# Input projection's head: one small load on ACT, the first norm's gains turned alone, the first weight tile split in halves, addresses moved by 128 bytes

## The chip, the cores and the metric

The kernel runs on one core of one Trainium2 chip. The metric is device time in microseconds of one execution of the whole program; the time before is the median of three runs, 1946.9 us (1945.45 to 1949.15).

## The reference, cut to what matters

One layer of a streaming encoder: a prompt of 1024 tokens and 8 samples of 16 tokens, width 1024, all in float32. The change touches only the first step, the norm and the projection into 3336 columns:

```python
def rmsnorm(x, g):
    xf = x.astype(jnp.float32)
    y = xf * lax.rsqrt(jnp.mean(xf * xf, axis=-1, keepdims=True) + EPS)
    return (y * g.astype(jnp.float32)).astype(x.dtype)

xn = rmsnorm(x, lw['norm_mix_g'])
(qkv_raw, z, a, b, sq, sk, sv, sc_b, sc_c, sc_h) = split_cols(xn @ lw['w_in'], IN_SIZES)
```

After it come the gated delta rule, a window attention, a short convolution, the output projection, an attention into 256 memory tokens and the feed-forward part; none of their code changes.

## The kernel before, in words

Tokens: 1152 rows (1024 of the prompt, 128 of the samples) lie as 9 row tiles of 128 rows (x0 to x8 below), in three groups of three. Each product is computed as three float32r matmuls, from a high and a low part of either factor (`w_hi`·`hi`, `w_hi`·`lo`, `w_lo`·`hi`, lines 920 to 923).

`in_projection` (line 646) walks over 25 column tiles of the weights; the first five are sc_c, sc_h, sc_b, sc_c, sc_h. A column tile has three pieces (one for each group of 384 tokens), a piece has 8 inner blocks k, and a block three matmuls, "a product" below. Tile 0 does the norm at the same time. The steps of this head, by engine:

- SP (lines 728 to 738) issues the loads in one fixed order: x0, x1, x2, weights 0, x3, x4, x5, weights 1, x6, x7, x8, the two halves of the feed-forward convolution's old rows (16 rows of 2816 floats each, at partitions 0 to 15 and 32 to 47), the old rows of the two other convolutions, and then, each after a split of weights, weights 2 and on.
- ACT (lines 1013 to 1016) first issues 18 small loads, all vectors of the layer (14 in `table`, 4 in `vectors`), then loads its table, and runs `InputNorm.on_scalar` (line 310): the sums of squares of x0, x1, x2 (`square`), one square root for the three (`lengths`), and then, for each of 24 blocks i = 8·group + k, `high_part(i)`. After blocks 0, 1, 2 come the squares of x3, x4, x5, and after 8, 9, 10 those of x6, x7, x8 (`SPREAD`).
- PE (line 906) first waits for all 18 small loads and turns them into columns (`turn_vectors`, line 788), then turns the 8 blocks of the first group (`first_third`), each of three transposes into one of four PSUM banks: block i waits until block i−4 is through `low_part`. Then tile 0's products begin; before product k of piece p, PE turns block 8p + k + 4 (`before_product`, line 272) and waits for the low part of its own block. After piece 0 and 1 it turns the old feed-forward rows, after piece 2 the other old rows (`beside`, line 880).
- DVE (line 1287) copies the turned vectors into `C.vec`, then runs `on_vector` (line 324): the reciprocal and three scalings of group 0 (`scale`), then 24 times `low_part`; before blocks 4 and 12 it scales groups 1 and 2, before blocks 12 and 20 it copies old feed-forward rows out. Only then it splits weights 2 (`weights_low`).
- POOL (line 1087) makes the identity, splits weights 0 (a copy and a subtraction over the whole tile), makes the masks and splits weights 1.

Every engine runs its instructions in this order; semaphores alone join them. SBUF tiles on the left side lie one behind the other in the order in which `program` (line 4322) makes them; weights of this projection lie on the right side.

Of the kernel before, what the change touches and what calls it, by code (L numbers as in the profile page):

```python
# [11 lines left out]
F32 = mybir.dt.float32  # L12
F32R = mybir.dt.float32r
ALU = mybir.AluOpType
# [3 lines left out]
P = 128  # L18
# [70 lines left out]
class Ctx:  # L89


    def __init__(self, nc, stack):
        self.nc, self.stack = nc, stack
# [105 lines left out]
class NormParts:  # L199
# [4 lines left out]
    def __init__(self, nc, C, ph, tag, src, sums, gain_col, hi, lo, xn, banks):  # L204
        self.nc, self.C, self.src, self.sums, self.gain_col = nc, C, src, sums, gain_col
        self.hi, self.lo, self.banks = hi, lo, banks
        self.xn = xn.rearrange("p (i t d) -> p i t d", i=2, t=self.GROUP)
        self.root, self.inv = (ph.sb(f"{tag}_{n}", [P, NT]) for n in ("root", "inv"))
# [71 lines left out]
class InputNorm(NormParts):  # L280


    SPREAD = {0: 3, 1: 4, 2: 5, 8: 6, 9: 7, 10: 8}

    def __init__(self, nc, C, ph, src, hi, lo, xn, banks, squares, landed, ready):
        super().__init__(nc, C, ph, "nx", src, C.h_sums, V_MIX, hi, lo, xn, banks)
        self.squares, self.landed, self.ready = squares, landed, ready
        self.summed, self.vec_copied = ph.sem("nx_summed"), ph.sem("nx_vec_copied")

    def square(self, act, t):  # L290
        act.wait_ge(self.landed[t], 16)
        if t:
            act.wait_ge(self.summed, t)
        self.nc.scalar.activation(self.squares, self.src[:, t, :], ACT.Square, accum_out=self.sums[:, t:t + 1]
                                  ).then_inc(self.summed, 1)

    def lengths(self, act, g):
        ts = slice(g * self.GROUP, (g + 1) * self.GROUP)
        act.wait_ge(self.summed, (g + 1) * self.GROUP)
# [10 lines left out]
    def on_scalar(self, act):  # L310
        act.wait_ge(self.ready, 1)
        for t in range(self.GROUP):
            self.square(act, t)
        self.lengths(act, 0)
        act.wait_ge(self.vec_copied, 1)
        for i in range(NP * KD):
            self.high_part(act, i)
            t = self.SPREAD.get(i)
            if t is not None:
                self.square(act, t)  # L320
                if t % self.GROUP == self.GROUP - 1:
                    self.lengths(act, t // self.GROUP)

    def on_vector(self, dve, copy_old):
        self.scale(dve, 0)
        dve.wait_ge(self.vec_copied, 1)
        for i in range(NP * KD):
            if i % KD == KD // 2:
                if i // KD:
                    copy_old(i // KD - 1)  # L330
                if i // KD + 1 < NP:
                    self.scale(dve, i // KD + 1)
            self.low_part(dve, i)


class Ahead:
# [153 lines left out]
class FeatureWeights:  # L490
# [155 lines left out]
def in_projection(nc, C, A, O, M, hi, lo, weights, spill, scratch, x_tiles):  # L646
# [20 lines left out]
    with C.phase() as ph:  # L667
# [28 lines left out]
        x_landed = [ph.sem(f"x_landed{t}") for t in range(NT)]  # L696
        x_rows = kv.rearrange("p a b -> p (a b)").rearrange("p (t d) -> p t d", d=D)
        norm = InputNorm(nc, C, ph, x_rows, hi, lo, mix_flat[:, 0:6 * D],
                         [sums[:, i, :] for i in range(NP)] + [state_out[:]], R.x_squares, x_landed, ready)
        table, vectors = vector_table(C, A, *R.vec_rows)  # L700
        staged = ph.sem("c_staged")
        stored = C.conv_stored
        (rows_landed, projected, act_freed, dve_freed, old_turned, old_copied, padded, conv_step, conv_done,
# [20 lines left out]
        def _(sp):  # L724
# [60 lines left out]

        @block.tensor
        def _(pe):
            def turn_vectors():
                pe.wait_ge(ready, 1)
                pe.wait_ge(loaded, 16 * (len(table) + len(vectors)))  # L790
                at = 0
                for rows in R.vec_rows:
                    n = rows.shape[0]
                    ins = nc.tensor.transpose(misc[:, at:at + n], rows, C.ident[0:n, 0:n])
                    at += n
                ins.then_inc(vec_turned, 1)

# [22 lines left out]
            def turn_state(m):  # L820

                W = 3 if m < 2 else 4
                pe.wait_ge(gathered, m + 1)
                if m:
                    pe.wait_ge(state_saved, m)
                nc.tensor.transpose(state_out[0:W - 1, 0:P], tail[:, m % 2, 24:24 + W - 1], C.ident[:])
                nc.tensor.transpose(state_out[0:NB * (W - 1), P:2 * P], tail[:, m % 2, 0:NB * (W - 1)],
                                    C.ident[:]).then_inc(state_turned, 1)
# [51 lines left out]
            def beside(n, piece):  # L880

                if n == 0:
                    if piece < 2:
                        turn_ffn_rows(piece)
                    else:
                        turn_old_rows()
                if piece == 0:
                    if n >= 1 and tiles[n - 1][0] == "sc_h":
                        turn_state(tiles[n - 1][1])
                if piece == 1:  # L890
                    if n >= 1 and tiles[n - 1][0] == "conv":
                        turn_state(padded_of["conv", tiles[n - 1][1]])
                    if n == FIRST:
                        turn_gates()
                    if n == FIRST + 1:
                        sum_gates()
                    if n == FIRST + 2:
                        turn_gc()
                    if 0 <= n - FIRST - 2 < 2 * HEADS:
                        sum_squares(n - FIRST - 2)  # L900
                for e in KK_AT.get((n - COVER, piece), ()):
                    kk(e)
                if 0 <= NP * (n - COVER) + piece - 4 < E_ALL:
                    turn_v(NP * (n - COVER) + piece - 4)

            turn_vectors()
            norm.first_third(pe)
            for n, (kind, i, cols) in enumerate(tiles):
                rows = sum(c for _, c in cols)
                pe.wait_ge(split, n + 1)  # L910
                for piece in range(NP):
                    if n:
                        if by_act[n - 1]:
# [3 lines left out]
                    for k in range(KD):  # L917
                        if n == 0:
                            norm.before_product(pe, piece, k)
                        for m, (w, x) in enumerate(((w_hi, hi), (w_hi, lo), (w_lo, hi))):  # L920
                            ins = nc.tensor.matmul(banks[0:rows, piece, 0:TC], w[:, n % 2, k, 0:rows],  # L921
                                                   x[:, k, piece * TC:piece * TC + TC], start=(k == 0 and m == 0),
# [9 lines left out]
        def _(act):  # L932
# [127 lines left out]
        def _(pool):  # L1060
# [63 lines left out]
        def _(dve):  # L1124
# [162 lines left out]
            dve.wait_ge(vec_turned, 1)  # L1287
            nc.vector.tensor_copy(C.vec[:], misc[:, 0:V_ALL]).then_inc(norm.vec_copied, 1)
# [3033 lines left out]
def program(nc, A, O):  # L4322
    with ExitStack() as stack:
# [155 lines left out]
```

## Time and profile before

| | |
|---|---|
| median of three runs | 1946.9 us |
| profiled execution | 1941.18 us |
| its span, first to last instruction | 1939.8 us |
| PE busy | 1851.0 us (95%) |
| DVE, ACT, POOL busy | 60%, 41%, 38% |
| mean granted clock of PE | 0.988 |

The span is what the trace covers; some 1.4 us of the profiled execution lie around it. Busy times of an engine are shares of that span. PE is busy nearly everywhere, so what matters is where it is not.

### The profile page before, as it was taken

The page shows a single profiled execution, that of the slowest core. Times are in us where ns is not written, and L with a number is a line of the kernel's source. Part 1 is how long each engine was busy: PE and PEld are TensorE (multiplying, and loading weights), DVE is VectorE, ACT ScalarE, POOL GpSimd, SP SyncE. Part 2 cuts the span into 40 slices and gives each one's busy share as a digit, 9 for nine tenths or more (in the row PEclk, how much of TensorE's full clock was granted, in tenths as well). Part 3 has the DMA queues.
Part 4 walks back from the last instruction along what each step waited for, and adds up shares of the span by engine and source line. Part 5 has one row for each costly group of instructions (what it writes and reads, how often), then busy time and mean ns, then how long its engine had stood idle before and what let it go on. Part 6 is the DMA issues. An engine that isn't in the chain of part 4 may idle for free. (4 is left out here: it accounts for less than half of the span.)

```text
span 1939.8 us, 27945 instructions
## 1 busy us (share of the span) xinstructions
PE 1851.0 (95%) x10427; PEld 1694.0 (87%) x10427; DVE 1162.3 (60%) x1367; ACT 788.0 (41%) x1499; POOL 737.4 (38%) x650
## 2 busy tenths in 40 slices
PE   5999999999989999999998997999999999999999
PEld 4989889998967788898887887999999999987787
DVE  4224555655656642423415148887788877699985
ACT  4104664315675442311124236444444444444432
POOL 3001212005434260121114305766666666547743
PEclk9999999999999999999999999999999999999999
DMA  6121212214133340112431122222222222496454
GB/s 165 36 57 35 59 35 56 70 59 138 55 120 120 120 176 22 44 66 92 172 117 55 55 66 77 77 68 68 78 68 77 69 68 68 156 340 205 160 172 142
DMA packets 159034, 188.07 MB, mean 97 GB/s; under 512 B 13809, under 2 KB 112730, under 8 KB 158520
## 3 DMA queue, kind: packets, MB, share of 16 engines
q1 hardware_dynamic: 157156, 186.30, 29.2%
q8 instruction: 65, 1.06, 0.2%
q10 hardware_dynamic: 884, 0.25, 0.1%
q0 software_dynamic: 896, 0.19, 0.0%
q14 instruction: 33, 0.27, 0.0%
HBM read 151.64 MB, written 35.07 MB: 96 GB/s over the span
## 5 line engine op out<-in xcount | busy, mean ns | idle before, releaser
L3573 PE MATMUL ffn_banks<-h_parts,up_hi 128*128 128x384 f32 x1920 | 496.5, 340 | 10.0 <-POOL h_parts L3977 4.3
L3573 PEld LDWEIGHTS ffn_banks<-h_parts,up_hi 128*128 128x128 f32 x1920 | 350.2, 189 | 11.4 <-issue 7.2
L3573 PE MATMUL ffn_banks<-h_parts,up_lo 128*128 128x384 f32 x960 | 325.4, 339 | 0.0
L3973 POOL TENSOR_TENSOR up_lo<-up_raw,up_hi 128x512 fp32r<-128x512 f32 x174 | 256.2, 1489 | 141.6 <-ACT up_hi L3735 141.5
L921 PE MATMUL proj_banks<-x_hi,in_w_hi 128*128 128x384 f32 (+1 forms) x648 | 225.6, 348 | 4.2 <-DVE room L1308 4.2
L921 PE MATMUL proj_banks<-x_lo,in_w_hi 128*128 128x384 f32 (+1 forms) x648 | 220.1, 340 | 0.0
L921 PE MATMUL proj_banks<-x_hi,in_w_lo 128*128 128x384 f32 (+1 forms) x648 | 219.8, 339 | 0.0
L3573 PEld LDWEIGHTS ffn_banks<-h_parts,up_lo 128*128 128x128 f32 x960 | 181.1, 189 | 0.0
L4024 POOL TENSOR_TENSOR h_parts<-down_cells,h_parts 128x512 fp32r<-128x512 f32 x69 | 111.0, 1616 | 92.7 <-ACT h_parts L3808 92.6
L3694 PE MATMUL ffn_banks<-h_parts,up_hi 128*128 128x512 f32 x352 | 140.0, 398 | 0.8 <-DVE h L4241 0.8
L3697 PE MATMUL ffn_banks<-h_parts,up_lo 128*128 128x512 f32 x352 | 138.9, 395 | 0.0
L3696 PE MATMUL ffn_banks<-h_parts,up_hi 128*128 128x512 f32 x352 | 138.8, 394 | 0.0
L921 PEld LDWEIGHTS proj_banks<-x_hi,in_w_hi 128*128 128x128 f32 (+1 forms) x648 | 120.5, 186 | 8.1 <-DVE in_w_lo L783 4.8
L3735 ACT ACTIVATE up_hi<-up_raw 128x512 fp32r<-128x512 f32 x176 | 105.3, 630 | 47.2 <-DVE up_raw L4052 37.8
L921 PEld LDWEIGHTS proj_banks<-x_lo,in_w_hi 128*128 128x128 f32 (+1 forms) x648 | 120.4, 186 | 3.1
L921 PEld LDWEIGHTS proj_banks<-x_hi,in_w_lo 128*128 128x128 f32 (+1 forms) x648 | 120.1, 185 | 2.1
L4052 DVE TENSOR_TENSOR up_raw<-up_raw 128x512 f32<-128x512 f32 x88 | 117.9, 1358 | 2.0
L1105 POOL MEMSET room<- 128x3 f32 (+1 forms) x14 | 1.4, 101 | 243.2 <-DVE room L1145 216.6
L783 DVE TENSOR_TENSOR in_w_lo<-in_w_raw,in_w_hi 128x1024 fp32r<-128x1024 f32 (+1 forms) x25 | 32.8, 1311 | 97.7 <-ACT in_w_hi L940 97.6
L4115 DVE SCALAR_TENSOR_TENSOR h<-h,vec 128x1168 f32<-128x1168 f32 x44 | 85.9, 1951 | 2.1 <-ACT h L3785 2.1
L4119 DVE SCALAR_TENSOR_TENSOR h<-h,vec 128x1168 f32<-128x1168 f32 x44 | 81.0, 1841 | 5.8 <-DVE h L4115 2.4
L3820 ACT ACTIVATE up_hi<-up_raw 128x640 fp32r<-128x640 f32 (+1 forms) x66 | 46.0, 701 | 90.1 <-DVE up_raw L4225 45.1
(515 smaller groups left out, 3918.2 us busy)
## 6 DMA issues: line engine op xcount, KB each, us to landing
up_raw<-in_w_up SPq DMA_DIRECT2D x44, 512.0 KB, 3.7
down_cells<-in_w_down SPq DMA_DIRECT2D x58, 256.0 KB, 5.7
up_raw<-ffn_gated_rows SPq DMA_DIRECT2D x44, 320.0 KB, 5.6
ffn_gated_rows<-h SPq DMA_DIRECT2D x22, 576.0 KB, 2.8
in_w_raw<-in_w_in SPq DMA_DIRECT2D x24, 512.0 KB, 3.7
up_raw<-ffn_gated_rows SPq DMA_DIRECT2D x44, 256.0 KB, 3.2
mem_k_one<-in_cache_mem_k SPq DMA_DIRECT2D x8, 1024.0 KB, 4.9
spill<-mixT SPq DMA_DIRECT2D x10, 576.0 KB, 3.8
```

What stands on the lines that cost most here:

```text
L921: ins = nc.tensor.matmul(banks[0:rows, piece, 0:TC], w[:, n % 2, k, 0:rows], x[:, k, piece * TC:piece * TC + TC], start=(k == 0 and m == 0 ...
L3573: ins = nc.tensor.matmul(banks[:, bank, 0:TC], wt[:, j, k, :], parts[:, q, x, k, :], start=(fresh and n == 1), stop=(n == last), skip_grou ...
L3694: nc.tensor.matmul(bank, a_hi[:, x_at, w_at], b_slot(n, 0), start=(i == 0 and not again), stop=False, skip_group_check=again)
L3696: nc.tensor.matmul(bank, a_hi[:, x_at, w_at], b_slot(n, 1), start=False, stop=False, skip_group_check=again)
L3697: ins = nc.tensor.matmul(bank, a_lo[:, x_at, w_at], b_slot(n, 0), start=False, stop=(i == STEPS - 1), skip_group_check=again)
L3735: nc.scalar.activation(w_hi[:, j], weights.full(j), ACT.Copy).then_inc(weights.high[j], 1)
L3820: nc.scalar.activation(a_hi[:, n % LEAD, 0:a_width(n)], a_cell(n), ACT.Copy).then_inc(a_high, 1)
L3973: nc.gpsimd.tensor_tensor(w_lo[:, j], weights.full(j), w_hi[:, j].bitcast(F32), ALU.subtract).then_inc(weights.split[j], 1)
L4024: nc.gpsimd.tensor_tensor(b_slot(n, 1), b_cell(n), b_slot(n, 0).bitcast(F32), ALU.subtract).then_inc(b_split, 1)
L4052: nc.vector.tensor_tensor(weights.full(j), x, z, op).then_inc(weights.formed[j], 1)
L4115: nc.vector.scalar_tensor_tensor(y[:, s, 0:LY], xp[:, s, 1:1 + LY], C.vec[:, col], y[:, s, 0:LY], ALU.mult, ALU.add).then_inc(conv_step, 1)
L4119: nc.vector.scalar_tensor_tensor(y[:, s, 0:LY], xp[:, s, 2:2 + LY], C.vec[:, col], y[:, s, 0:LY], ALU.mult, ALU.add).then_inc(conv[s], 1)
```

## The change

It does these things, all in the input projection's head but for the last:

1. ACT issues one load alone, the gains of this norm (`table[0]`); the other 17 small loads go to SP's queue, behind x8.
2. PE turns these gains alone (`turn_mix_gains`) before the first group; the other vectors are turned into the bank `state_out` after piece 0 of tile 1, and DVE copies them between the old rows' copy and the split of weights 2.
3. The loads of the old feed-forward rows go from behind x8 to in front of weights 1.
4. The squares are shared: ACT has x0 to x3, x5, x6, x8, DVE has x4 (after low part 1) and x7 (after low part 9).
5. DVE scales the next group before low parts 5 and 13 (was 4 and 12), and PE turns one block less ahead (k + 3 for k + 4).
6. POOL splits weights 0 in two halves of four blocks each; tile 0 starts on the first half.
7. The norm uses `C.root` and `C.inv` for its own two small tiles, and an unused tile of 128 bytes per partition, `level`, is put behind `eps`, so that the left side's later tiles lie 128 bytes higher.

```diff
+    ON_SCALAR, ON_VECTOR = {1: 3, 4: 5, 8: 6, 10: 8}, {1: 4, 9: 7}
+    SCALE_AT = KD // 2 + 1
...
+    def square_dve(self, dve, t):
+        dve.wait_ge(self.landed[t], 16)
+        if t > self.GROUP + 1:
+            dve.wait_ge(self.summed_dve, t // self.GROUP - 1)
+        self.nc.vector.scalar_tensor_tensor(self.junk, self.src[:, t, :], 1.0, self.src[:, t, :], ALU.mult, ALU.mult,
+                                            accum_out=self.sums[:, t:t + 1]).then_inc(self.summed_dve, 1)
...
         for i in range(NP * KD):
-            if i % KD == KD // 2:
-                if i // KD:
-                    copy_old(i // KD - 1)
-                if i // KD + 1 < NP:
-                    self.scale(dve, i // KD + 1)
+            if i % KD == KD // 2 and i // KD:
+                copy_old(i // KD - 1)
+            if i % KD == self.SCALE_AT and i // KD + 1 < NP:
+                self.scale(dve, i // KD + 1)
             self.low_part(dve, i)
+            t = self.ON_VECTOR.get(i)
+            if t is not None:
+                self.square_dve(dve, t)
+
+    def before_product(self, pe, p, k):
+        i = KD * p + k + KD - self.SCALE_AT
...
+    def split_halves(self, nc, pool, high, split):
+        self.wait(pool, 0)
+        for i, (to_high, to_split) in enumerate(((high, split), (self.high, self.split))):
+            ks = slice(i * KD // 2, (i + 1) * KD // 2)
+            nc.gpsimd.tensor_copy(self.hi[:, 0, ks], self.raw[:, 0, ks]).then_inc(to_high, 1)
+            pool.wait_ge(to_high, 1)
+            nc.gpsimd.tensor_tensor(self.lo[:, 0, ks], self.raw[:, 0, ks], self.hi[:, 0, ks].bitcast(F32), ALU.subtract
+                                    ).then_inc(to_split, 1)
...
-            for s in range(2):
-                sp.dma_start(ffn_rows[s], A["state_ffn_conv"][0].rearrange("b i c -> (b i) c")[:, FF * s:FF * s + FF]
-                             ).then_inc(ffn_landed, 16)
+                if n == 0:
+                    for s in range(2):
+                        sp.dma_start(ffn_rows[s], A["state_ffn_conv"][0].rearrange("b i c -> (b i) c")[:, FF * s:FF * s + FF]
+                                     ).then_inc(ffn_landed, 16)
+            for to, frm in table[1:] + vectors:
+                sp.dma_start(to, frm).then_inc(loaded, 16)
...
+            def turn_mix_gains():
+                pe.wait_ge(ready, 1)
+                pe.wait_ge(mix_landed, 16)
+                nc.tensor.transpose(misc[:, V_MIX:V_MIX + KD], table[0][0], C.ident[0:KD, 0:KD]).then_inc(mix_turned, 1)
...
                 if piece == 0:
+                    if n == 1:
+                        turn_vectors()
...
-            turn_vectors()
+            turn_mix_gains()
             norm.first_third(pe)
...
-            for to, frm in table + vectors:
-                act.dma_start(to, frm).then_inc(loaded, 16)
+            act.dma_start(*table[0]).then_inc(mix_landed, 16)
...
-            weights.split_first(nc, pool, 0)
+            weights.split_halves(nc, pool, half_high, half_split)
...
+            dve.wait_ge(vec_turned, 1)
+            nc.vector.tensor_copy(C.vec[:, mix.stop:], state_out[:, mix.stop:V_ALL]).then_inc(rest_copied, 1)
+            dve.wait_ge(rest_copied, 1)
             for n, (kind, i, cols) in enumerate(tiles):
...
+        C.sb("level", [P, 32])
```

## Rows read from the trace of the kernel before

**Rows 1.** The page's part 1: busy us (share of the span) xinstructions.
```profile
PE 1851.0 (95%) x10427; PEld 1694.0 (87%) x10427; DVE 1162.3 (60%) x1367; ACT 788.0 (41%) x1499; POOL 737.4 (38%) x650
```
**Rows 2.** PE's waits, 0 to 90 us: waited for: us, times, longest.
```profile
PE misc L794 <- DMA sinks<-in_swa_sinks: 15.9, 1, 15.9
PE proj_banks L921 <- DVE room L1308: 3.0, 1, 3.0
```
**Rows 3.** Timeline, ACT: start, us, instruction [idle before <-releaser].
```profile
8.09 0.45 ACTq L1014 DMA_DIRECT2D sinks<-in_swa_sinks  x1
8.57 1.28 ACT L1015 ACT_TABLE_LOAD   x1 [8.57 <-issue]
9.87 1.06 ACT L294 ACTIVATE room<-kv 128x1024 f32<-128x1024 f32 x1
...
13.53 0.30 ACT L300 ACTIVATE nx_root<-h_sums,eps 128x3 f32<-128x3 f32 x1
```
**Rows 4.** Timeline: the vectors' turn, then scalings, turns and high part of group 0.
```profile
15.92 0.80 PE L794 MATMUL misc<-ident,room 91*128 91x91 f32 x3 [15.92 <-DMA sinks<-in_swa_sinks]
...
17.27 2.14 DVE L226 TENSOR_SCALAR mixT<-kv,nx_inv 128x1024 f32<-128x1024 f32 x3
...
19.46 2.18 PE L239 MATMUL norm_sums<-ident,mixT 128*128 128x128 f32 x9 [2.75 <-DVE mixT L226]
...
20.46 0.58 ACT L246 ACTIVATE x_hi<-norm_sums,vec 128x384 fp32r<-128x384 f32 x1 [6.63 <-PE norm_sums L239]
```
**Rows 5.** DMA issue to landing: x0 to x2; x3 to x5; x6 to x8; weights 0; feed-forward rows.
```profile
DMA to landing us min/median/max: 3.7/4.5/6.2
...
DMA to landing us min/median/max: 9.1/9.5/10.3
...
DMA to landing us min/median/max: 11.4/12.8/12.9
...
DMA to landing us min/median/max: 8.3/8.3/8.3
...
DMA to landing us min/median/max: 11.8/13.1/14.4
```
**Rows 6.** Timeline, PE in tile 0 and at the start of tile 1.
```profile
27.07 0.67 PE L921 MATMUL proj_banks<-x_hi,in_w_hi 128*128 128x384 f32 x1
...
28.17 0.52 PE L921 MATMUL proj_banks<-x_hi,in_w_hi 128*128 128x384 f32 x1
...
34.22 1.53 PE L807 MATMUL misc<-ident,mixT 16*128 16x16 f32 x22
...
40.62 0.52 PE L239 MATMUL norm_sums<-ident,mixT 128*128 128x128 f32 x3 [1.31 <-DVE x_lo L251]
...
45.66 0.55 PE L239 MATMUL norm_sums<-ident,mixT 128*128 128x128 f32 x3
...
52.34 0.44 PE L921 MATMUL proj_banks<-x_hi,in_w_hi 128*128 128x384 f32 x1
```
**Rows 7.** Windows: stretch, PE, PEld, DVE, ACT, POOL busy, PEclk, DMA share, GB/s.
```profile
25.00:30.00 5.00, 3.68 (x15) 3.47 (x15) 4.04 (x8) 2.86 (x8) 1.35 (x1) 0.69 1.06 192
```
**Rows 8.** DMA part, 20.0 to 24.7 us, when the old rows were moved.
```profile
DMA packets 286, 0.48 MB, mean 101 GB/s; under 512 B 48, under 2 KB 238, under 8 KB 266
```
**Rows 9.** Timeline: splits of weights 0 and 2, weights 3's high part.
```profile
11.69 2.35 POOL L534 TENSOR_TENSOR in_w_lo<-in_w_raw,in_w_hi 128x1024 fp32r<-128x1024 f32 x1
...
52.94 1.23 DVE L783 TENSOR_TENSOR in_w_lo<-in_w_raw,in_w_hi 128x1024 fp32r<-128x1024 f32 x1
...
65.37 1.06 ACT L940 ACTIVATE in_w_hi<-in_w_raw 128x1024 fp32r<-128x1024 f32 x1 [12.46 <-PE proj_banks L921]
```
**Rows 10.** Groups by line: count | busy us, mean ns | idle.
```profile
L921 PE MATMUL proj_banks<-x_lo,in_w_hi 128*128 128x384 f32 (+1 forms) x648 | 220.1, 340 | 0.0
L921 PE MATMUL proj_banks<-x_hi,in_w_lo 128*128 128x384 f32 (+1 forms) x648 | 219.8, 339 | 0.0
...
L2324 DVE SCALAR_TENSOR_TENSOR swa_att<-swa_work,hide 128x1024 f32<-128x1024 f32 x9 | 11.0, 1219 | 20.4 <-PE swa_work L2224 9.1 <-PE swa_work L2229 6.0 <-PE swa_work L2226 5.3
```

More of the change, by code:

```diff
@@ L207, in __init__ @@
         self.xn = xn.rearrange("p (i t d) -> p i t d", i=2, t=self.GROUP)
-        self.root, self.inv = (ph.sb(f"{tag}_{n}", [P, NT]) for n in ("root", "inv"))
+        self.root, self.inv = C.root, C.inv
         self.rooted, self.inverted, self.scaled, self.turned, self.high, self.low = (
@@ L280, with __init__ @@
 class InputNorm(NormParts):
-    SPREAD = {0: 3, 1: 4, 2: 5, 8: 6, 9: 7, 10: 8}
-    def __init__(self, nc, C, ph, src, hi, lo, xn, banks, squares, landed, ready):
+    ON_SCALAR, ON_VECTOR = {1: 3, 4: 5, 8: 6, 10: 8}, {1: 4, 9: 7}
+    SCALE_AT = KD // 2 + 1
+    def __init__(self, nc, C, ph, src, hi, lo, xn, banks, squares, junk, landed, ready):
         super().__init__(nc, C, ph, "nx", src, C.h_sums, V_MIX, hi, lo, xn, banks)
-        self.squares, self.landed, self.ready = squares, landed, ready
-        self.summed, self.vec_copied = ph.sem("nx_summed"), ph.sem("nx_vec_copied")
+        self.squares, self.junk, self.landed, self.ready = squares, junk, landed, ready
+        self.summed, self.summed_dve, self.vec_copied = (ph.sem(f"nx_{n}") for n in ("summed", "summed_dve", "vec_copied"))
+        self.count = 0
     def square(self, act, t):
@@ L292, in square @@
         if t:
-            act.wait_ge(self.summed, t)
+            act.wait_ge(self.summed, self.count)
+        self.count += 1
         self.nc.scalar.activation(self.squares, self.src[:, t, :], ACT.Square, accum_out=self.sums[:, t:t + 1]
                                   ).then_inc(self.summed, 1)
+    def square_dve(self, dve, t):
[4 more added lines that the diff above has]
+                                            accum_out=self.sums[:, t:t + 1]).then_inc(self.summed_dve, 1)
     def lengths(self, act, g):
         ts = slice(g * self.GROUP, (g + 1) * self.GROUP)
-        act.wait_ge(self.summed, (g + 1) * self.GROUP)
+        act.wait_ge(self.summed, self.count)
+        if g:
+            act.wait_ge(self.summed_dve, g)
         self.nc.scalar.activation(self.root[:, ts], self.sums[:, ts], ACT.Sqrt, scale=1.0 / D, bias=self.C.eps[:, 0:1]
@@ L317, in on_scalar @@
             self.high_part(act, i)
-            t = self.SPREAD.get(i)
+            t = self.ON_SCALAR.get(i)
             if t is not None:
@@ L325, in on_vector @@
         self.scale(dve, 0)
-        dve.wait_ge(self.vec_copied, 1)
         for i in range(NP * KD):
-            if i % KD == KD // 2:
-                if i // KD:
-                    copy_old(i // KD - 1)
-                if i // KD + 1 < NP:
-                    self.scale(dve, i // KD + 1)
-            self.low_part(dve, i)
+            if i % KD == KD // 2 and i // KD:
+                copy_old(i // KD - 1)
+            if i % KD == self.SCALE_AT and i // KD + 1 < NP:
+                self.scale(dve, i // KD + 1)
+            self.low_part(dve, i)
+            t = self.ON_VECTOR.get(i)
[3 more added lines that the diff above has]
+        i = KD * p + k + KD - self.SCALE_AT
+        if KD <= i < NP * KD:
+            self.turn(pe, i)
+        pe.wait_ge(self.low, KD * p + k + 1)
 class Ahead:
@@ L698, in in_projection @@
         norm = InputNorm(nc, C, ph, x_rows, hi, lo, mix_flat[:, 0:6 * D],
-                         [sums[:, i, :] for i in range(NP)] + [state_out[:]], R.x_squares, x_landed, ready)
+                         [sums[:, i, :] for i in range(NP)] + [state_out[:]], R.x_squares, R.y[:, 0:D], x_landed, ready)
         table, vectors = vector_table(C, A, *R.vec_rows)
+        mix_landed, mix_turned, half_high, half_split, rest_copied = (ph.sem(f"s0_{n}") for n in (
+            "mix_landed", "mix_turned", "half_high", "half_split", "rest_copied"))
         staged = ph.sem("c_staged")
@@ L787, in _ @@
         def _(pe):
+            def turn_mix_gains():
+                pe.wait_ge(ready, 1)
+                pe.wait_ge(mix_landed, 16)
+                nc.tensor.transpose(misc[:, V_MIX:V_MIX + KD], table[0][0], C.ident[0:KD, 0:KD]).then_inc(mix_turned, 1)
             def turn_vectors():
-                pe.wait_ge(ready, 1)
-                pe.wait_ge(loaded, 16 * (len(table) + len(vectors)))
+                pe.wait_ge(loaded, 16 * (len(table) - 1 + len(vectors)))
                 at = 0
@@ L793, in turn_vectors @@
                     n = rows.shape[0]
-                    ins = nc.tensor.transpose(misc[:, at:at + n], rows, C.ident[0:n, 0:n])
+                    ins = nc.tensor.transpose(state_out[:, at:at + n], rows, C.ident[0:n, 0:n])
                     at += n
@@ L825, in turn_state @@
                     pe.wait_ge(state_saved, m)
+                else:
+                    pe.wait_ge(rest_copied, 1)
                 nc.tensor.transpose(state_out[0:W - 1, 0:P], tail[:, m % 2, 24:24 + W - 1], C.ident[:])
@@ L909, in _ @@
                 rows = sum(c for _, c in cols)
-                pe.wait_ge(split, n + 1)
+                if n == 0:
+                    pe.wait_ge(half_split, 1)
+                else:
+                    pe.wait_ge(split, n + 1)
                 for piece in range(NP):
@@ L919, in _ @@
                             norm.before_product(pe, piece, k)
+                            if piece == 0 and k == KD // 2:
+                                pe.wait_ge(split, 1)
                         for m, (w, x) in enumerate(((w_hi, hi), (w_hi, lo), (w_lo, hi))):
@@ L1285, in copy_ffn_rows @@
                 nc.vector.tensor_copy(M["ffn_old"][:, NF * s:NF * s + NF, :], ffn_bank).then_inc(ffn_copied, 1)
-            dve.wait_ge(vec_turned, 1)
-            nc.vector.tensor_copy(C.vec[:], misc[:, 0:V_ALL]).then_inc(norm.vec_copied, 1)
+            mix = slice(V_MIX, V_MIX + KD)
+            dve.wait_ge(mix_turned, 1)
+            nc.vector.tensor_copy(C.vec[:, mix], misc[:, mix]).then_inc(norm.vec_copied, 1)
+            dve.wait_ge(norm.vec_copied, 1)
             norm.on_vector(dve, copy_ffn_rows)
```

## The prediction

> **What bounds the kernel now.** I read the page's head and engine table first: PE is busy 1851.0 us, 95% of the span, so time is to be had only where PE stands idle or is slow [rows 1]. Next came the waits of PE in the first 90 us: 15.9 us for the landing of `sinks`, the last of ACT's 18 small loads, and 3.0 us for DVE at the head of tile 2 [rows 2]. No product runs before 27.07, and tile 1 starts at 52.34 [rows 6]; tile 0 and its head are the only part that this change can shorten. From there on the order is as before and each engine waits for another one, for nothing tied to the clock on the wall, so I take it that a tile 1 that starts earlier ends the program earlier by as much.
>
> Then the timeline engine by engine. ACT issues loads until 8.54, loads its table until 9.85, and does three squares, the root ending at 13.83 [rows 3]. But x0, x1, x2, issued at 0.8, 1.3 and 1.8, had landed 3.7, 4.5 and 6.2 us after issue, at 4.5, 5.8 and 8.0 [rows 5]. DVE could scale from 13.85; it waits for the vectors, which PE turns at 15.92 to 16.72, and starts scaling at 17.27; PE turns the first block at 19.46, and the first high part starts at 20.46 [rows 4]. So two delays stand in a row: ACT starts late, and the vectors land later still.
>
> **Part by part, on the path.** All times are in the profiled execution.
>
> *One load on ACT.* ACT's issue ends at 1.42, its table load (1.28) at 2.7. Squares cost 1.22 to 1.25 each (three from 9.87 to 13.53), and each now waits for its tile: x0 4.5 to 5.8, x1 5.8 to 7.0, x2 8.0 to 9.25 [rows 3, 5]. Root at 9.45 to 9.75, reciprocal 0.2, three scalings 2.14: first turn at 12.2 for 19.46, 7.3 us earlier. The gains' load leaves first of all, at 0.82, like x0, and is needed only by 12.2; I take its turn and copy at nothing. If it took as long as `sinks` did (8.09 to 15.9, 7.8 us) it would still be there at 8.6.
>
> *First group.* From the first turn to the first high part is 1.0 us, to the first low part 1.7. ACT then does high 0, 1 (0.5 each where they follow one another), square x3, high 2, 3, 4, square x5, the second root; before, three squares lay between highs 0 to 3. A DVE square with its sum is not in the trace: the same kind of operation over 1024 elements took 1.22 [rows 10]. Below I see no reason for less than 1.1 (ACT's own is 1.06); above, twice an ACT square, 2.5. I take 1.25, the near row. In order: high 0 13.2, high 1 14.3, square x3 until 15.6, highs 2, 3, 4 until 17.2, square x5 until 18.4, root 18.7. DVE: lows 0, 1 until 15.1, square x4 until 16.4, lows 2, 3, 4 until 18.1, scale group 1 from 18.8 to 21.1, lows 5, 6, 7 until 22.8. PE: turn 6 waits for low 2 (17.0), turn 7 for low 3 (17.6), product 0 starts at 18.0 for 27.07, nine us earlier.
>
> *Halves of weights 0.* Weights 0 land at 10.5 [rows 5] and POOL had split the whole tile at 14.04, four us before 18.0 [rows 9]. The halves buy nothing at either start; their two extra instructions, some 0.3 us, end by 14.5 and cost nothing. Only with a start before 14 would the half split matter.
>
> *Clock.* Before, the first products ran at a granted clock of 0.50, that is 1.2 of 2.4 GHz: product 1 starts 1.1 us behind product 0 (27.07, 28.17), and a mean of 0.69 over 25 to 30 is some 3.1 us at half speed, after a stretch in which PE did only scattered turns [rows 6, 7]. At full speed a product's three matmuls take 0.53 (its mean matmul of 0.34 overlaps the next by half), at half speed I take 0.96. Those scattered turns stay, so I expect the slow stretch again: ten matmuls slow and five fast, products 0 to 4 from 18.0 to 22.1. Bounds: full clock, where group 1's scaling (21.1) binds, 1.0 earlier; all five slow, 0.7 later. From there a product with its turn costs 0.85 (40.62 to 45.66 holds four and old-row turns of 1.53 [rows 6]): piece 0 ends at 24.7, its old-row turns (1.5) at 26.3.
>
> *Feed-forward rows before weights 1.* They are needed at 24.7. Behind x5 (14.6) they should land at about 18 and 21, at the spacing of 3.0 us between the two in the row; nothing waits. But weights 1, x6, x7, x8 stand behind them now. While old rows moved, the 16 engines carried 101 GB/s [rows 8]. The pair is 352 KB, 360,000 bytes, so 3.6 us at that rate, less 0.7 for the small loads' 250 KB (by their shapes) that no longer lie in front, at the 1.4 us that x3 to x5 took for 512 KB each. x6, x7 had landed at 18.6 and 20.0 and x8 only at 24.7 [rows 5], because the old rows came right behind it; now small loads do. At the pace of the others it would have landed at 21.5 to 22.7; with the 2.9 on top I take x6 at 21.5 and x8 at 25.6. Bounds: x8 at 24.4 (2.9 on 21.5) and 30.7 (both full spacings, 6.0, on its old landing).
>
> The Trainium skill ("SBUF — State Buffer", section on the DMA port swizzle) says that DMA bandwidth depends on how many of 16 SBUF ports the partitions reach; 16 neighbouring partitions reach four. By its 436 GB/s the pair would run at 109 GB/s and take 3.3 us, which goes with the 101 GB/s of the row, but not with 6.0; by it x8 would come at 25.3 and the sum would be better by 0.3. Either way it speaks against putting these loads ahead of anything wanted soon.
>
> *Second and third group.* High 8 ends at 23.3, square x6 at 24.5, highs 9 and 10 at 25.5, square x8 from 25.6 to 26.9; DVE does low 9, square x7 until 27.0; root 27.4. High 11 stands behind the square on ACT, so low 11 ends at 28.6, then the old rows' copy (0.5), low 12 until 29.7, and group 2's scaling until 32.0. PE reaches its wait for that scaling at turn 16, now before product 5 of the piece, about 30.4, and stands 1.6 us, much as before at product 4 (1.31 in front of 40.62 [rows 6]). Piece 1 ends at 34.9, its old-row turns at 36.6; piece 2 with the other old rows had taken 6.7 us (45.66 to 52.34) and has one turn more (0.3): tile 1 starts at 43.6 for 52.34, that is 8.7 less.
>
> *The moved vectors.* Three turns now lie inside tile 1: they took 0.80 us [rows 4]. Between 0.3 (at the 0.07 us of one old-row turn, 22 in 1.53, and a little for their size) and 1.1 (the 0.80 and a pause around them), I take 0.6. DVE waits for them before splitting weights 2, which in before's times then ends some 4.8 us later than 54.17 [rows 9]; behind it stand only the split of weights 3, whose high part waits for tile 1's end (65.37) anyway, and SP's load of weights 4, wanted after tile 2. Tile 2 can't start before 65.3, so six us of cover are left. On SP, 17 issues of 0.42 us (as on ACT, 8.54 less 1.42) stand before the old rows and weights 2, whose issue so goes back to about 21; behind the old rows of 160 KB it lands before 32; ACT wants it at 43. Covered by 10 us.
>
> *Addresses.* Only left-side tiles move, by 128 bytes. The trace shows no effect of an address: two groups of projection matmuls whose operands lie in different places have means of 340 and 339 ns [rows 10]. That 1 ns over 1944 matmuls is ±1.9 us; I take 0.
>
> **Sum.** 8.7 − 0.6 = 8.1 us off the profiled execution (1941.18 to 1933.1; span to 1931.7). The shown median stands 5.7 above that execution, so 1946.9 − 8.1 = 1938.8 us.
>
> **Rivals.**
> - *Late row tiles.* The moved rows hold x6 to x8 up by their full spacing. x8 lands at 30.7, root 32.5, group 2 scaled at 37; piece 1 ends near 39.5 for 34.9. Off come 8.1 − 4.6 = 3.5 us: 1943.4. For it: spacing 3.0 each. Against: 101 GB/s, and part of that spacing was other rows.
> - *More.* Full clock at the first products and x8 at 24.4: about 1.5 us more, and up to the 1.9 us by addresses: 1935.4 to 1937.3.
> - *Gain given back.* A later stage depends on a transfer or on POOL in a way that the shift upsets. Nothing in the waits shows it; 3.0 us for DVE at tile 2 stays either way. At all 8.1 lost 1946.9, at five 1943.8; I count 1945.
> - *Slower: addresses.* x_hi and x_lo, the moving operand of all 1944 projection matmuls, shift against the weights on the right. At 0.176 us from one to the next, 2.4% more, 4.2 ns each, eats the 8.1 us; from there it is slower. At 5% the result is 1955. Against it: the 1 ns between those two groups [rows 10].
> - The halves doing nothing is part of the forecast, not a rival; were they the point of the change, it would be worth 0.
>
> **How the numbers follow.** Forecast 0.56 (1936.5 to 1941.5), late tiles 0.16, more 0.12, given back 0.08, slower 0.08. What a measurement can tell from no change is 0.2%, 3.9 us: faster means below 1943.0. Late tiles fall on both sides of that, two thirds faster. Faster 0.56 + 0.12 + 0.11 = 0.79; same 0.05 + 0.08 = 0.13; slower 0.08. The range from 1934.0 to 1944.5 leaves out most of the slower case, the far end of late tiles and a little beyond "more".
>
> **What would show it.** Root at 9.5 to 10, first turn near 12.2, first product near 18, with the clock at 0.50 there; x8's square at 25 to 26 on ACT with no or a short wait; a wait of PE for group 2's scaling near 30 to 32; tile 1 at 43 to 44; three turns inside it; no wait at weights 2. Wrong if high 9 or 11 stands long behind a square that waits for a load, if the first product still starts beyond 22, or if the spacing of matmuls in later tiles differs from 0.176.

## The result, and the profile after

The changed kernel takes 1925.1 us (median of 4 runs, 1924.4 to 1927.2) beside 1946.2 us (1944.7 to 1949.2) for the kernel before on the same chip: a ratio of 0.9896 [0.9881, 0.9910], by which it takes 20.2 us less (17.5 to 23.2 by the interval). The forecast was 8.1 us less, and 1925.1 lies below its range, which ends at 1934.0. The profiled execution took 1924.76 us, 16.4 less than the profiled one of before, which itself lay 5 us under its median.

Part 1 of the page of after, beside [rows 1]: busy us, share, instructions.

```profile
PE 1837.0 (96%) x10428; PEld 1682.3 (87%) x10428; DVE 1173.3 (61%) x1372; ACT 785.9 (41%) x1495; POOL 737.1 (38%) x652
```

PE is busy 14.0 us less for one instruction more. A shorter wait at the head doesn't make an engine less busy; nine slow matmuls in the head (below) account for some 1.4 us of it. So most of the 14 has to be matmuls that are shorter. PE's waits of after, 0 to 90 us, beside [rows 2]:

```profile
PE norm_sums L239 <- DVE mixT L226: 11.4, 3, 9.4
PE misc L824 <- POOLq L1131: 3.7, 1, 3.7
PE proj_banks L967 <- DVE room L1358: 3.0, 1, 3.0
```

The wait for `sinks` is gone, and of the 11.4 us for scalings 9.4 now stand before the first turn, which starts at 13.34 and waits for DVE's first three scalings. Before it PE waits 3.7 us for POOL's identity. The 3.0 us at tile 2 stayed.

Timeline of after, start of the head, beside [rows 3, 4, 6, 9]: start, us, instruction.

```profile
1.45 1.28 ACT L1060 ACT_TABLE_LOAD   x1 [1.45 <-PEq L4519]
...
8.84 0.30 ACT L312 ACTIVATE h_root<-h_sums,eps 128x3 f32<-128x3 f32 x1
...
9.46 3.82 DVE L226 TENSOR_SCALAR mixT<-kv,h_inv 128x1024 f32<-128x1024 f32 x3
10.14 1.58 POOL L555 TENSOR_TENSOR in_w_lo<-in_w_raw,in_w_hi 128x512 fp32r<-128x512 f32 x1
...
11.67 1.07 POOL L553 CAST in_w_hi<-in_w_raw 128x512 fp32r<-128x512 f32 x1
...
13.34 2.18 PE L239 MATMUL norm_sums<-ident,mixT 128*128 128x128 f32 x9 [9.36 <-DVE mixT L226]
...
18.83 0.42 PE L967 MATMUL proj_banks<-x_hi,in_w_hi 128*128 128x384 f32 x1
19.09 0.34 PE L967 MATMUL proj_banks<-x_lo,in_w_hi 128*128 128x384 f32 x1
```

The root is 0.6 us earlier than forecast; three scalings that took 2.14 [rows 4] take 3.82 beside POOL's split; the first product starts at 18.83 (forecast 18.0, before 27.07), the second matmul 0.26 behind it and the next ones 0.17 apart: no half speed. The same view, second group and start of tile 1:

```profile
25.26 1.53 PE L844 MATMUL misc<-ident,mixT 16*128 16x16 f32 x22
25.34 1.06 ACT L297 ACTIVATE room<-kv 128x1024 f32<-128x1024 f32 x1
25.43 2.37 POOL L562 TENSOR_TENSOR in_w_lo<-in_w_raw,in_w_hi 128x1024 fp32r<-128x1024 f32 x1
25.55 3.33 DVE L304 SCALAR_TENSOR_TENSOR room<-kv 128x1024 f32<-128x1024 f32 x1
...
28.99 0.30 ACT L312 ACTIVATE h_root<-h_sums,eps 128x3 f32<-128x3 f32 x1 [2.50 <-DVE room L304]
...
33.61 0.55 PE L239 MATMUL norm_sums<-ident,mixT 128*128 128x128 f32 x3 [1.40 <-DVE mixT L226]
...
45.05 0.44 PE L967 MATMUL proj_banks<-x_hi,in_w_hi 128*128 128x384 f32 x1
...
49.32 0.51 PE L831 MATMUL state_out<-ident,room 91*128 91x91 f32 x3
```

The square of x7 on DVE takes 3.33 us beside POOL's subtraction, which started first; that of x4, which started ahead of a small mask of POOL, took 1.23. ACT waits 2.50 for it. Tile 1 starts at 45.05 for 52.34 [rows 6], and the three vector turns inside it take 0.51: the head gives 7.3 − 0.5 = 6.8 us. Nothing in the head explains the other 9.6 us between the two profiled executions. They lie in stages whose code is untouched. One line by itself, first of after, then of before (duration of one: min/median/max ns, first and last start in us), for the feed-forward product of 384 columns:

```profile
L3623 PE MATMUL ffn_banks<-h_parts,up_hi x1920: 334/334/686, 1149.4 to 1670.3; 128*128 128x384 f32 x192
```
```profile
L3573 PE MATMUL ffn_banks<-h_parts,up_hi x1920: 336/337/658, 1158.1 to 1684.0; 128*128 128x384 f32 x192
```

The median matmul is 3 ns shorter, and this stage runs 520.9 us for 525.9. (A matmul overlaps the next: by the starts in the two traces the median step from one to the next is 173 ns for 175.) By the same starts, tile 1 to the end of the projection takes 373.7 for 376.0 (and holds the 0.5 of turns), and the feed-forward's second half, from 1670.6 to 1918.9 for 1684.4 to 1935.2, 248.3 for 250.8. Between projection and feed-forward part it takes 730.6 for 729.8. The groups of after by line, beside [rows 10]: count | busy us, mean ns | idle.

```profile
L967 PE MATMUL proj_banks<-x_hi,in_w_lo 128*128 128x384 f32 (+1 forms) x648 | 217.5, 336 | 0.0
L967 PE MATMUL proj_banks<-x_lo,in_w_hi 128*128 128x384 f32 (+1 forms) x648 | 217.3, 335 | 0.0
...
L3747 PE MATMUL ffn_banks<-h_parts,up_lo 128*128 128x512 f32 x352 | 137.1, 390 | 0.0
```
```profile
L3697 PE MATMUL ffn_banks<-h_parts,up_lo 128*128 128x512 f32 x352 | 138.9, 395 | 0.0
```

The second fence is of before: 395 to 390 ns there, 340 and 339 to 335 and 336 in the projection. The only part of the change that reaches these stages, other than that they start earlier, is the shift by 128 bytes.

### The profile page after: what moved, and what is told of

Its sections match the earlier page's. It is cut to its first block and busy times, and to the rows that moved or that the text cites. A ratio compares the mean times of both kernels' runs of the same rounds, so it can differ in the third digit from the quotient of the medians.

```text
span 1923.5 us, 27954 instructions
## 1 busy us (share of the span) xinstructions
PE 1837.0 (96%) x10428; PEld 1682.3 (87%) x10428; DVE 1173.3 (61%) x1372; ACT 785.9 (41%) x1495; POOL 737.1 (38%) x652
## 5 line engine op out<-in xcount | busy, mean ns | idle before, releaser
L3623 PE MATMUL ffn_banks<-h_parts,up_hi 128*128 128x384 f32 x1920 | 491.6, 337 | 11.1 <-POOL h_parts L4027 4.3
L3623 PEld LDWEIGHTS ffn_banks<-h_parts,up_hi 128*128 128x128 f32 x1920 | 348.6, 189 | 12.4 <-issue 7.3
L3744 PEld LDWEIGHTS ffn_banks<-h_parts,up_hi 128*128 128x128 f32 x352 | 66.1, 188 | 18.2 <-DVE h L4291 3.2
```

The source lines that it names most:

```text
L3623: ins = nc.tensor.matmul(banks[:, bank, 0:TC], wt[:, j, k, :], parts[:, q, x, k, :], start=(fresh and n == 1), stop=(n == last), skip_grou ...
L3744: nc.tensor.matmul(bank, a_hi[:, x_at, w_at], b_slot(n, 0), start=(i == 0 and not again), stop=False, skip_group_check=again)
```

## The experiments

Theory A: the head gives about 7 us, and the rest is the shift, because the time of a matmul depends on the distance between the addresses of its two SBUF operands (the weights that are loaded into PE, and the data of 384 columns that are moved past them). Rivals: B, all of it starts in the head (a later stage profits from the shift in time); C, what counts is where the left-side tiles lie, or the norm's small tiles.

The addresses follow from adding up the tiles in the order in which they are made. `x_hi` starts at byte 94048 of its partition before and 94176 after, `in_w_hi` at 184288 in both: a distance of 90240 before (128 over a multiple of 256) and 90112 after (a multiple of 256). `up_hi` and `h_parts` likewise go from 128 over to a multiple. The operands of the memory queries don't move, those of the two output projections (`wo`, `mo`) move together, and all of them have a multiple of 256 in both kernels; they kept their medians (334 and 389 ns).

**e1: the head without the shift.** The changed kernel less one line; the norm keeps `C.root` and `C.inv`.

```diff
-        C.sb("level", [P, 32])
```

> The changed kernel without the 128-byte tile, so every left tile is where it was before. Theory A (addresses): the head brings its 7 us and nothing else; about 1939 to 1940 us, first matmul of tile 1 near 45, and the matmuls of the projection and of the feed-forward part back at medians of 337 ns (384 columns) and 395 (512). Theory B (the head brings everything, the rest by later overlaps): about 1925, as the changed kernel.

Measured: 1937.1 (1934.4 to 1940.7) beside 1948.1, ratio 0.9948 [0.9933, 0.9964], 10.1 us less. Tile 1 starts at 45.45. Its feed-forward groups:

```profile
L3623 PE MATMUL ffn_banks<-h_parts,up_lo 128*128 128x384 f32 x960 | 325.2, 339 | 0.0
...
L3747 PE MATMUL ffn_banks<-h_parts,up_lo 128*128 128x512 f32 x352 | 138.9, 395 | 0.0
```

The head as in after, the matmuls as in before. B falls: the later stages don't profit from an earlier start.

**e2: the shift without the head.** The kernel before, with:

```diff
-        self.root, self.inv = (ph.sb(f"{tag}_{n}", [P, NT]) for n in ("root", "inv"))
+        self.root, self.inv = C.root, C.inv
...
+        C.sb("level", [P, 32])
```

> The kernel before, with nothing but the 128-byte tile behind eps (and the norm's two tiny tiles taken from C, so that it fits). Theory A: projection and feed-forward matmuls at 334 and 390 ns; 1944 x 2.1 ns + 2880 x 2.7 ns + 1056 x 6 ns is up to 18 us, of which waits give some back: 1930 to 1935 us, tile 1 still starting at 52.3. Theory B: 1946, no change.

Measured: 1933.9 (1931.4 to 1936.8), ratio 0.9929 [0.9916, 0.9943]: 13.8 us less, although tile 1 started at 54.82 in its profiled execution (`sinks` landed at 17.2). Its groups:

```profile
L3573 PE MATMUL ffn_banks<-h_parts,up_lo 128*128 128x384 f32 x960 | 322.2, 336 | 0.0
L921 PE MATMUL proj_banks<-x_hi,in_w_hi 128*128 128x384 f32 (+1 forms) x648 | 223.8, 345 | 4.2 <-DVE room L1308 4.2
...
L3697 PE MATMUL ffn_banks<-h_parts,up_lo 128*128 128x512 f32 x352 | 137.1, 390 | 0.0
```

The smaller edit is worth more than the head. The two parts add up to 23.9 us for the 20.2 of after and the 21.8 of e3, within their intervals. Some of e1's 10.1 isn't the head: its trace has the head at 6.9 us with the vector turns still to come inside tile 1, and its six executions had a mean granted clock of 0.9875, the eleven of before beside them 0.9852, which is worth up to 4.5 us of 1937.

**e3: the shift on the other side.** The left side stays as in e1, and the weights on the right move by 128.

```diff
-        C.sb("level", [P, 32])
+        C.sb("level", [P, 32], side="right")
```

> The changed kernel with the 128-byte tile on the right side: left tiles as before, right ones 128 bytes lower. Theory A1 (what counts is the distance between the weights' and the data's address, which is a multiple of 256 bytes again): 1925 us, 334 and 390 ns. Theory A2 (where the left tiles themselves lie counts): 1939 us, 337 and 395 ns, as without the tile.

Measured: 1927.0 (1922.5 to 1928.6), ratio 0.9888 [0.9870, 0.9907]; 336, 390 ns, as after. C falls: the left tiles lie where they did in e1, and the time is that of after; the distance decides.

**e4 and e5: 64 and 32 bytes.** Distances 64 and 96 over a multiple of 256.

```diff
-        C.sb("level", [P, 32])
+        C.sb("level", [P, 16])
```

> The changed kernel with a 64-byte tile: distance between weights and data 64 bytes off a multiple of 256 (128 off before, 0 in the changed kernel). A smooth effect of the distance: half of the gain, about 1932 us, medians between 334 and 337. If only 0 is fast: 1939 us. If only 128 is slow: 1925.

> The changed kernel with a tile of 32 bytes: distance 96 off a multiple of 256. Medians at 0, 64, 128 off were 334, 336, 337 (384 columns) and 390, 392, 395 (512). If it grows evenly: 337 and 393 to 394.

e5 has `[P, 8]` in that line. e4: 1928.2 (1927.3 to 1930.8), ratio 0.9906 [0.9889, 0.9922]; the even growth that was expected would have given 1932. e5: 1938.3, one execution, beside 1948.5. In the feed-forward part the median of the 384-column kind is 334 ns at distance 0, 336 at 64, 338 at 96, 337 at 128; of the 512-column kind 389, 392, 392 to 399, 393. Its 384-column stage took 520.9, 520.1, 529.2 and 524.6 to 526.9 us, so there 64 costs nothing and 96 more than 128. The projection goes another way, first of e5 (96), then of after (0):

```profile
L967 PE MATMUL proj_banks<-x_hi,in_w_hi x648: 332/336/637, 19.2 to 418.1; 128*128 128x384 f32 x156, 128*8 128x384 f32 x6
```
```profile
L967 PE MATMUL proj_banks<-x_hi,in_w_hi x648: 332/334/637, 18.8 to 418.8; 128*128 128x384 f32 x156, 128*8 128x384 f32 x6
```

From tile 1 on that is 372.8 us in e5 (tile 1 at 45.28) for 373.7 in after: at 96 the projection has the full gain. The two stages lie opposite ways round: in the projection the weights have the higher address, in the feed-forward part the data. So between the multiples of 256 it matters which operand lies higher, or something else in which the two stages differ; this stays open. Only 0 and 128 are alike in both.

**e7 and e8: the same cost made elsewhere.** A gap of 128 and of 256 bytes between weights and activations of `wo` and `mo` in the changed kernel; e8 has `[P, 64]`.

```diff
         w_hi, w_lo = ph.sb(f"{tag}_w_hi", [P, KD, D], F32R), ph.sb(f"{tag}_w_lo", [P, KD, D], F32R)
+        ph.sb(f"{tag}_gap", [P, 32])
```

> The changed kernel with 128 unused bytes between weights and data of the two output projections, both on the left side, nothing else moved against the other. Distance rule: their 828 matmuls of 512 columns go from a median of 389 ns to 394 or 395, the stretch of each projection from 96.0 us to about 98.4; projection and feed-forward matmuls stay at 334 and 390. If left against right matters and not the distance: 389 ns, 96.0 us.

> The same with 256 bytes. If what counts is the distance modulo 256, everything as in the changed kernel, 389 ns and 96.0 us; if any distance that isn't a multiple of more (512, 1024) is slow, 394 and 98.4.

Measured: e7 1932.0, e8 1924.6, one execution each. The line of `wo` and `mo` in e7, then in e8 (as above for the feed-forward line):

```profile
L2675 PE MATMUL wo_banks<-wo_w_lo,wo_act_hi x138: 387/393/404, 676.5 to 774.7; 128*128 128x512 f32 x138
...
L2675 PE MATMUL mo_banks<-mo_w_lo,mo_act_hi x138: 387/393/404, 1051.3 to 1149.4; 128*128 128x512 f32 x138
```
```profile
L2675 PE MATMUL wo_banks<-wo_w_lo,wo_act_hi x138: 389/389/395, 675.1 to 771.2; 128*128 128x512 f32 x138
...
L2675 PE MATMUL mo_banks<-mo_w_lo,mo_act_hi x138: 389/389/393, 1046.8 to 1142.8; 128*128 128x512 f32 x138
```

128 bytes make either stage 2.1 us longer (98.2 and 98.1 for 96.1 and 96.0), 256 bytes nothing. So the effect appears and goes, as the theory says, on stages that the change never touched: 128 over a multiple of 256 is slow, another 128 is fast again. The rest of e7's 7.3 us over e8 lies elsewhere; its trace has PE at 1.2 GHz for 65 us behind tile 1's start, that of e8 for 53.

**c1: the kernel before once more**, to see how far one profiled execution repeats.

> The kernel before, looked at once more. Its three profiled heads so far put the landing of the last small load at 15.9 and, in the run with only the tile added, at 17.2, and tile 1 at 52.3 and 54.8. If that landing varies from run to run, tile 1 starts somewhere from 52 to 56 here, as much after its landing (36.4 to 37.6 us) as in those two, and matmul medians are 337 and 395 ns again.

1944.1; `sinks` at 15.94, tile 1 at 52.12, medians 337 and 393 ns: the readings of before repeat. The later start that e2 had for `sinks` (17.2) did not come again.

**h1: the square of x7 on ACT.** After block 9, in place of DVE's.

```diff
-    ON_SCALAR, ON_VECTOR = {1: 3, 4: 5, 8: 6, 10: 8}, {1: 4, 9: 7}
+    ON_SCALAR, ON_VECTOR = {1: 3, 4: 5, 8: 6, 9: 7, 10: 8}, {1: 4}
...
-        if g:
-            act.wait_ge(self.summed_dve, g)
+        if g == 1:
+            act.wait_ge(self.summed_dve, 1)
```

> The changed kernel with x7's square on ACT behind high part 9, where DVE had it beside POOL's split of weights 1 and took 3.33 us for it. If the collision is the price: DVE is free 3.3 us earlier, ACT is 1.25 later, the root comes at 27.8 for 29.0, group 2 is scaled a good microsecond earlier and tile 1 starts near 44 for 45.05; 1924 us. If the root isn't what PE waits for: 45.05 again.

Measured: 1923.9 (1922.0 to 1925.8), ratio 0.9872 [0.9853, 0.9890]. Its timeline:

```profile
27.23 0.30 ACT L312 ACTIVATE h_root<-h_sums,eps 128x3 f32<-128x3 f32 x1
...
31.86 0.55 PE L239 MATMUL norm_sums<-ident,mixT 128*128 128x128 f32 x3 [0.96 <-DVE mixT L226]
...
43.28 0.44 PE L967 MATMUL proj_banks<-x_hi,in_w_hi 128*128 128x384 f32 x1
```

The root comes 1.8 us earlier and tile 1 too (43.28 for 45.05). The step is shown in the trace; in the whole time it is not: between the ratios of h1 and of after, 0.2% apart, the intervals overlap.

**h2: the feed-forward rows back behind x8.** The two loads are issued after the loop over n.

```diff
-                if n == 0:
-                    for s in range(2):
-                        sp.dma_start(ffn_rows[s], ...
+            for s in range(2):
+                sp.dma_start(ffn_rows[s], ...
```

> The changed kernel with the feed-forward rows' loads back behind x8. PE wants these rows at 25.3; before they landed at 24.1 and 27.1. Theory: PE waits for them some 1 to 2 us at the end of piece 0, tile 1 starts at 46 to 47 for 45.05, although x6 to x8 land earlier, since nothing waited for those. Rival (late tiles cost more than the rows win): 45 or earlier.

Measured: 1927.1, one execution. The rows are turned at 25.46 with no wait, and tile 1 starts at 45.24. So the expectation of 46 to 47 failed, and its rival held: moving these loads brings nothing at the faster head, and costs nothing either.

**h3: weights 0 split whole.**

```diff
-            weights.split_halves(nc, pool, half_high, half_split)
+            weights.split_first(nc, pool, 0)
```

> The changed kernel with weights 0 split whole, as before. Product 0 starts at 18.8, the whole split ends near 13 to 14: no effect on PE, tile 1 at 45.0 give or take 0.3. Possible gain: POOL is done earlier, so less of it lies beside DVE's first scalings (3.82 us for the three in the changed kernel, 2.14 before): up to 1 us earlier.

Measured: 1920.4, one execution. Its timeline:

```profile
9.95 5.04 DVE L226 TENSOR_SCALAR mixT<-kv,h_inv 128x1024 f32<-128x1024 f32 x3
11.01 2.66 POOL L562 TENSOR_TENSOR in_w_lo<-in_w_raw,in_w_hi 128x1024 fp32r<-128x1024 f32 x1
...
25.70 2.37 POOL L562 TENSOR_TENSOR in_w_lo<-in_w_raw,in_w_hi 128x1024 fp32r<-128x1024 f32 x1
26.64 2.52 DVE L304 SCALAR_TENSOR_TENSOR room<-kv 128x1024 f32<-128x1024 f32 x1
```

With one long subtraction on POOL the scalings take 5.04 us for 3.82, and the first turn comes 1.7 later, at 15.04. The gain of up to 1 us that was held possible was a loss. By tile 1 (45.31 for 45.05) only 0.3 of it is left, as the second scalings take 2.08 us for 2.68 and the x7 square meets less of POOL's second subtraction. Its total lies 4.7 us under the profiled execution of after; that isn't the head but goes with the granted clock: behind tile 1's start the trace has PE at 1.2 GHz for 38.5 us, that of after for 48.1, and half of the difference is 4.8.

**h4: the small loads on ACT's queue again**, 17 of them behind the gains.

```diff
-            for to, frm in table[1:] + vectors:
-                sp.dma_start(to, frm).then_inc(loaded, 16)
...
             act.dma_start(*table[0]).then_inc(mix_landed, 16)
+            for to, frm in table[1:] + vectors:
+                act.dma_start(to, frm).then_inc(loaded, 16)
```

> The changed kernel with the other 17 small loads on ACT again (the gains still turned alone). ACT issues until 8.5, its first square starts at 9.9 and the root ends at 13.8; the first turn is then near 16.1, for 13.34 in the changed kernel and 19.46 before: this part of the change is worth 2.8 us, the turning of the gains alone 3.3. Tile 1 near 47.5. If x loads decided, it would stay at 45.

Measured: 1925.0, one execution. Its timeline:

```profile
12.96 0.30 ACT L312 ACTIVATE h_root<-h_sums,eps 128x3 f32<-128x3 f32 x1
...
13.58 2.67 DVE L226 TENSOR_SCALAR mixT<-kv,h_inv 128x1024 f32<-128x1024 f32 x3
...
22.54 2.13 DVE L226 TENSOR_SCALAR mixT<-kv,h_inv 128x1024 f32<-128x1024 f32 x3
...
26.26 2.38 POOL L562 TENSOR_TENSOR in_w_lo<-in_w_raw,in_w_hi 128x1024 fp32r<-128x1024 f32 x1
...
27.96 1.76 DVE L304 SCALAR_TENSOR_TENSOR room<-kv 128x1024 f32<-128x1024 f32 x1
```

The root is 4.1 us later than after's, the first turn 3.0 (16.30, as expected), tile 1 only 0.8 (45.88, where 47.5 was expected). Of the 4.1, 1.2 come back where the scalings meet less of POOL (2.67 for 3.82), the rest mostly at the second group, which is scaled without POOL beside it (2.13 for 2.68) and whose x7 square takes 1.76 for 3.33. So of the 7.3 us most are there even with all the loads on ACT: what frees the head is that the first turn no longer waits for the last of 18 loads.

## Why the prediction was wrong

**The step that failed is *Addresses*.** It said "The trace shows no effect of an address: two groups of projection matmuls whose operands lie in different places have means of 340 and 339 ns", and took 0 with bounds of ±1.9 us. Measured: 13.8 us by e2, 11.1 to 16.4 by its interval. Two things were missed. First, the two groups were no test: `x_lo` lies 36,864 bytes above `x_hi`, `in_w_lo` 16,384 below `in_w_hi`, both multiples of 256, so all of them had the same distance modulo 256. The test was in the same trace: memory queries, 384 columns like the projection, stood at 334 ns where the projection's median was 337:

```profile
L2824 PE MATMUL mq_banks<-hn_hi,mq_w_hi x184: 334/334/426, 788.5 to 895.1; 128*128 128x384 f32 x184
```

Second, the step counted 1944 projection matmuls only, though left-side tiles are operands in every later stage. Between the two single profiles the projection's share is 2.7 us (2.2 shorter with 0.5 of turns inside) and the feed-forward part's 5.0 + 2.5. The sign that the prediction had named came: the step from matmul to matmul in the later tiles is 173 ns for 175. Of the 5 ns per step in the second half of the feed-forward part (227 for 232) half does not arrive: PE idles 3.5 us before its first kind for 0.8 before, nearly all for DVE, which is then the slower one.

That these single profiles give 10 us and the medians 13.8 goes in part with the granted clock, which fell oftener in the faster one: in the 384-column stage PE was at 1.2 GHz for 10.2 us in after and for 6.8 in before. An estimate takes half of such time off, for which the slow first products speak (steps of 0.32 us for 0.17). Then the three traces at distance 128 (before, e1, c1) have medians of 374.6, 522.0 and 251.9 us for the projection without turns, the 384-column stage and the second half, and the nine at distance 0 have 371.8, 515.8 and 248.7: together 12 us, inside e2's interval.

The rival *Slower: addresses* had the right mechanism and the wrong sign: it was priced as a loss only, and *More* held the gain down to the 1.9 us.

**One load on ACT, first group:** right in kind. Root 8.84 for 9.45; the first turn 13.34 for 12.2, since three scalings cost 3.82 and not 2.14; first product 18.83 for 18.0. The x4 square took 1.23, as taken (1.25).

**Halves:** "buy nothing" holds nearly at tile 1 (0.3 us by h3). What was missed is that they shorten the collision of POOL with DVE's scalings by 1.2 us.

**Clock:** the slow stretch was expected again and did not come; this hid a part of the losses. The granted clock in 18 to 25, where the first products now run, is 1.00 in after; before, in 25 to 30, it was 0.69 [rows 7]:

```profile
18.00:25.00 7.00, 6.38 (x39) 5.76 (x39) 5.84 (x10) 4.81 (x11) 6.09 (x15) 1.00 1.01 306
```

Behind the first matmul one follows each 0.17 to 0.18 us, in all kernels with the new head. In before and e2, where 7.6 us or more with scattered turns stood between the first turn and the first product, and not 5.4 to 5.8, the first nine (before, 1.4 us lost) and twelve (e2) are followed at 0.32 to 0.47: 1.2 GHz for 2.4. In e2 the row of the granted clock shows no fall there (1.00 in 25 to 30), so the spacing is the better witness. What decides was not tried by itself.

**Feed-forward rows, late tiles:** the loads did no harm. They landed within 12.3 us of issue at 4.5 and 5.0, by 17.4, not 18 and 21; x8 came 12.3 us after its issue at 11.0, at 23.3 for the 25.6 taken, and ACT squared it at 25.34 without a wait. The rival *Late row tiles* falls; h2 shows the order of these loads to be worth nothing.

**Second and third group:** the square of x7 was taken until 27.0 and ended at 28.9. Root 28.99 for 27.4, turn 16 at 33.61, tile 1 at 45.05 for 43.6: that is the 1.5 us by which the head falls short, and h1 gets 1.8 of it back.

The Trainium skill ("SBUF — State Buffer", section "SBUF: two separate sides") says that a DVE instruction with two SBUF inputs and a GpSimd one that reads SBUF exclude one another for a whole instruction, and that the one that starts first has its way. The trace agrees: in after, h3 and h4 the square ends 1.08 or 1.09 us after POOL's subtraction does, wherever it began (28.88 after 27.80, 29.16 after 28.07, 29.72 after 28.64). In the other order it is POOL that waits: the x4 square began at 16.07 and took its 1.23, and a mask of POOL that takes 0.31 elsewhere (h4) took 1.16 and ended 0.17 behind it.

```profile
16.31 1.16 POOL L167 TENSOR_SCALAR_AFFINE_SELECT block_mask<-block_mask 128x128 f32<-128x128 f32 x1
```

By that rule an estimate for the x7 square, from its 1.23 us alone, is an end 1.2 us behind POOL's subtraction, given when that starts.

**The moved vectors:** 0.51 for 0.6, and no wait at weights 2, as forecast. **Sum of the head:** 6.8 in the trace, 10.1 [7.0, 13.1] by e1's ratio, 8.1 forecast. **Given back:** nothing that can be shown. After takes 0.8 us more between the projection and the feed-forward part, but PE was at 1.2 GHz there for 30.7 us, and for 27.3 in before, which alone is worth up to 1.7.

## What to carry to other kernels

An edit that moves an address is an edit of every stage behind it: list the operand pairs it touches with their distance modulo 256 before pricing it, and compare groups of one shape that differ in that distance. Put the two SBUF operands of a matmul of this kind (float32r, 128 columns of weights, 384 or 512 of data) a multiple of 256 bytes apart; on either side of it only 128 over is known to cost in every stage that was tried. When two profiles differ by a few us, compare the time that each spent at the lower clock before looking for a cause. Before a reduction goes to DVE, look at what POOL does in that window and which of the two starts first; an instruction of 1.2 us took 3.3 behind a POOL subtraction.

## What was not expected of the hardware

- Matmul time by distance of the operands modulo 256, feed-forward part: 334, 336, 338, 337 ns (384 columns) and 389, 392, 392 to 399, 393 ns (512) at 0, 64, 96, 128 bytes; projection: 334, 335, 336, 337 ns, and no loss in the stage's time at 96, nor at 64 once half of the time at 1.2 GHz is taken off. 32 was not run.
- The 72 projection matmuls with only 8 columns of weights gained nothing: means of 335 to 336 ns at 128 (before), 337 at 0 (after).
- POOL's half split takes longer too when DVE scales beside it: its subtraction 1.58 us for 1.27 and its copy 1.07 for 0.61 in h4, where DVE was idle.
- First products at 0.32 us spacing with a recorded granted clock of 1.00 (e2).
